# Two edits in the expert loops of a two-block transformer kernel: the order in which u and v are asked for, and the order of a tile's score products

## The chip, the core and the metric

The kernel runs on one core of a Trainium2 chip. The metric is the device time of one execution in microseconds (us), lower is better. The core has five engines with instruction streams of their own: TensorE (PE, matmuls), VectorE (DVE), ScalarE (ACT), GpSimd (POOL) and SyncE (SP), which here issues all transfers. They wait for each other by semaphores. Each engine works its stream off in order, SyncE's queue too: a transfer whose wait has not ended holds up all transfers behind it.

## What is computed

The reference runs two blocks over 256 tokens of width 1024 in float32. Nearly half of the kernel's time, and all of the change, lies in the expert layers ("PEER") of the second block, which has two:

```python
def block(x_t):
    q = jnp.einsum('td,dhk->thk', x_t, w_q).reshape(T, PEER_HEADS, 2, PEER_HALF)
    s = jnp.einsum('thpk,hpnk->thpn', q, sub_keys).astype(jnp.float32)
    sv, si = lax.top_k(s, K)
    ...
    gate = jax.nn.softmax(fv, axis=-1)
    u = u_emb[eidx]
    v = v_emb[eidx]
    act = jax.nn.gelu(jnp.einsum('thkd,td->thk', u, x_t).astype(jnp.float32), approximate=False)
    return jnp.einsum('thk,thkd->td', (gate * act).astype(x_t.dtype), v)
```

Each token picks 8 x 16 of 16384 experts. The kernel does not gather: it computes the scores of all 16384 experts, multiplies them by a gate that is zero where an expert was not picked, and adds up all values. The 16384 experts are 128 tiles of 128, and a tile has two matrices of 128 x 1024 float32 (512 KB), u for the scores and v for the values.

## The kernel before

To keep float32's precision with rounded operands (fp32r), each operand is split into a high part (the rounded copy) and a low part (the rest), and a product is made of high x high, high x low and low x high.

The first 26 tiles of a layer (EARLY) get their scores ahead of time. From tile 26 on, all engines run a software pipeline, written as a loop of six tiles (STEP) a turn. For tile j:

- TensorE: `expert_scores(j)` (L813) makes 16 matmuls into one PSUM bank. L819 multiplies u's high part by both parts of the activations at once (512 columns, the "merged" product), L820 u's low part by their high part (256 columns). `expert_values(j)` (L823) makes 12 matmuls of 512 columns by `in_parts` (L507). The order is scores of j+1, values of j, scores of j+2, values of j+1, and so on. The end of scores adds 1 to `expert_scored`, the end of values adds 1 to `expert_used`.
- ScalarE: after scores of j it stores half of them (L1229), makes the high part of u of tile j+2 when that has landed (L1232), applies Gelu to tile j (L1234), and, when the values of j-1 have ended and v of j+1 has landed, makes the high part of that v (L1238).
- VectorE: the low part of v (L1832), the sum of the two halves of the scores (L1922), the low part of u of j+2 (L1832), and the product with the gate and its split into two parts (L1929, L1828, L1832), which lets the values of j start.
- SyncE: u and v have three slots each (E_SLOTS). u of tile n waits until the scores of n-3 are done (L2189) and is issued at L2190, v of tile n waits until the values of n-3 are done (L2196) and is issued at L2197. The low part of u is written in place of u and read by the scores, so the end of scores is what frees the slot.

The order of the transfers is written out by hand in `load_experts` (L2178), and the order in which TensorE multiplies in `expert_scores`.

Of the kernel before, what the change touches and what calls it, by code (L numbers as in the profile page):

```python
# [18 lines left out]
P = 128  # L19
D = 1024  # L20
KT = D // P
# [11 lines left out]
TILES = NKEYS  # L33
# [16 lines left out]
E_SLOTS = 3  # L50
STEP = 6
# [10 lines left out]
EARLY = CHOICE_TILES + GATE_TILES  # L62
# [55 lines left out]
def low_in_place(n):  # L118

    return n == 0 or n >= EARLY - 2  # L120
# [4 lines left out]
def program(nc, d, out):  # L125
    ctx = ExitStack()
    with ctx:
# [5 lines left out]
        def sem(name):  # L133
            if name not in sems:
                sems[name] = ctx.enter_context(nc.semaphore(name))
            return sems[name]
# [48 lines left out]
        def r3(a, n):  # L185
            return a.rearrange("p (a b) -> p a b", a=n)
# [224 lines left out]
        n = 0  # L411
# [79 lines left out]
        def _(pe):  # L491
# [236 lines left out]
            def experts(l):  # L728
# [24 lines left out]
                for h in range(HEADS8):  # L753
                    if h < PLAIN_HEADS:
                        name, j = ("pq", l, h // 2), h % 2
# [57 lines left out]
                def expert_scores(j, ready):  # L813

                    pe.wait_ge(sem("expert_u"), ready)
                    t = ps[:, 4 + j % 2, :]
                    for k in range(KT):
                        c = slice(k * P, (k + 1) * P)
                        pe.matmul(r3(t, 2), exp_uh[:, j % 2, c], ht_both[:, :, k, :], start=(k == 0), stop=False)  # L819
                        mm = pe.matmul(t[:, 0:T], exp_ul[:, j % E_SLOTS, c], ht_high[:, k, :], start=False, stop=(k == KT - 1))  # L820
                    mm.then_inc(sem("expert_scored"), 1)

# [13 lines left out]
                base = l * TILES  # L836
                for n in range(EARLY - 1):
                    expert_values(n, base + n + 1, first=(n == 0), low=None if low_in_place(n) else exp_uh[:, n % 2])
                    if n == G2_AT:
# [3 lines left out]
                        mm.then_inc(sem("g2_spread"), 1)  # L843
                pe.wait_ge(sem("ht_split"), l + 1)
                expert_scores(EARLY, l * LATE + 1)
                expert_values(EARLY - 1, base + EARLY)
                turns = (LATE - 2) // STEP
                with pe.Fori(0, turns) as i:
                    for j in range(STEP):
                        n = EARLY + j  # L850
                        expert_scores(n + 1, i * STEP + (l * LATE + j + 2))
                        expert_values(n, i * STEP + (base + n + 1))
                for n in range(EARLY + turns * STEP, TILES):
                    if n + 1 < TILES:
                        expert_scores(n + 1, l * LATE + n + 2 - EARLY)
                    expert_values(n, base + n + 1, last=(n == TILES - 1))
# [1301 lines left out]
        def _(sp):  # L2158
# [18 lines left out]
            def load_experts(l):  # L2177
                base = l * TILES  # L2178
                base_v = l * (TILES + 1)
                u, v = d["experts_u"][l], d["experts_v"][l]  # L2180

                def fetch_early(n):
                    if n >= P_SLOTS:
                        sp.wait_ge(sem("expert_scored"), base + n - P_SLOTS + 1)
                    sp.dma_start(pre_u[:, n % P_SLOTS], u[n]).then_inc(sem(f"early_u{n % P_SLOTS}_arrived"), 16)

                def fetch_u(s, src, free=None):
                    if free is not None:
                        sp.wait_ge(sem("expert_scored"), free)  # L2189
                    sp.dma_start(exp_u[:, s, :], src).then_inc(sem(f"expert_u{s}_arrived"), 16)  # L2190

                def fetch_v(s, src, free=None, split=None):
                    if split is not None:
                        sp.wait_ge(sem("expert_v"), split)
                    if free is not None:
                        sp.wait_ge(sem("expert_used"), free)  # L2196
                    sp.dma_start(exp_v[:, s, :], src).then_inc(sem(f"expert_v{s}_arrived"), 16)  # L2197

                def chunk_read(i):
                    s, v = released[("pq", l, i)]  # L2200
                    sp.wait_ge(s, v)

                chunk_read(1)
                chunk_read(2)
                U_AT = [FIRST + GATE_TILES + E_SLOTS + i for i in (0, 2, 4)]
                for n in range(P_SLOTS // 2):
                    fetch_early(n)
                chunk_read(3)
                for n in range(P_SLOTS // 2, P_SLOTS):
                    fetch_early(n)  # L2210
                for n in range(E_SLOTS):
                    fetch_v(n, v[VALUES[n]])
                for n in range(P_SLOTS, EARLY):
                    fetch_early(n)
                for n in range(E_SLOTS, EARLY):
                    if low_in_place(n - E_SLOTS):
                        fetch_v(n % E_SLOTS, v[VALUES[n]], base_v + n - E_SLOTS + 2)
                    else:
                        fetch_v(n % E_SLOTS, v[VALUES[n]], split=base + n - E_SLOTS + 1)
                    if n in U_AT:  # L2220
                        j = EARLY + U_AT.index(n)
                        sp.wait_ge(sem("early_read"), l + 1)
                        fetch_u(j % E_SLOTS, u[j])
                turns = LATE // STEP - 1
                for n in range(EARLY, EARLY + STEP):
                    if n >= EARLY + E_SLOTS:
                        fetch_u(n % E_SLOTS, u[n], base + n - E_SLOTS + 1)
                    if n - E_SLOTS < EARLY - 2:
                        fetch_v(n % E_SLOTS, v[n], split=base + n - E_SLOTS + 1)
                    else:  # L2230
                        fetch_v(n % E_SLOTS, v[n], base_v + n - E_SLOTS + 2)
                with sp.Fori(1, turns + 1) as i:
                    for j in range(STEP):
                        n, s = EARLY + j, (EARLY + j) % E_SLOTS
                        at_ = bass.ds(i * STEP + n, 1)
                        fetch_u(s, u[at_].rearrange("o p n -> (o p) n"), i * STEP + (base + n - E_SLOTS + 1))
                        fetch_v(s, v[at_].rearrange("o p n -> (o p) n"), i * STEP + (base_v + n - E_SLOTS + 2))
                sp.wait_ge(sem("expert_used"), (l + 1) * (TILES + 1))

            def load_keys(l):  # L2240
# [21 lines left out]
            for i in range(2, len(STREAM)):  # L2262
                name = STREAM[i]
                if name == ("evs",):
                    sp.wait_ge(sem("x_ready"), X_READY["end1"])
                    sp.dma_start(pool_mat.rearrange("p s g t -> p (s g t)"), d["pool"]).then_inc(sem("pool_mat"), 16)
                    sp.dma_start(tri_2, d["masks"][:, 4 * T:4 * T + P]).then_inc(sem("pool_mat"), 16)
                if name == ("evs",):
                    for _ in range(BLOCKS_BEHIND[("pool",)]):
                        fetch_block()  # L2270
                    load_keys(0)
                if name == ("od", SLOTS):
                    sp.wait_ge(sem("x_ready"), X_READY["peer_0"])
                    load_keys(1)
                if name == ("wcq",):
                    sp.wait_ge(sem("stored"), STORED["cv"])
                    sp.dma_start(c_row, d["c_row"]).then_inc(sem("c_loaded"), 16)
                load(i)
                for _ in range(BLOCKS_BEHIND.get(name, 0)):
                    fetch_block()  # L2280
                if name in (("pq", 0, 3), ("pq", 1, 3)):
                    load_experts(name[1])
                if name == ("pq", 0, 3):
                    sp.dma_start(causal_3.rearrange("p b k -> p (b k)"), d["masks"][:, 0:2 * T]).then_inc(sem("consts3"), 16)
                    sp.dma_start(inv_f, d["inv_f"]).then_inc(sem("consts3"), 16)
                    sp.dma_start(lam_in.rearrange("p a n -> p (a n)"), d["lam"]).then_inc(sem("consts3"), 16)
# [128 lines left out]
```

## Time and profile before

| | |
|---|---|
| time, median of 3 runs | 2500.53 us (2499.58 to 2501.54) |
| the profiled execution | 2501.91 us, its span 2500.1 us |
| granted TensorE clock | 0.991 of full speed |
| busy | PE 2392.6 us, DVE 1777.2, ACT 1018.3, POOL 298.8 |
| HBM read | 427.66 MB, 171 GB/s over the span |

The span goes from the first to the last instruction. Start times of matmuls are recorded, their ends are modelled: a matmul's recorded duration reaches past the start of the next, so the step from start to start tells the throughput. Times on a timeline are us from the start of the span. PEld is the load of weights, which overlaps matmuls.

### The profile page before, as it was taken

The page shows a single profiled execution, that of the slowest core. Times are in us where ns is not written, and L with a number is a line of the kernel's source. Part 1 is how long each engine was busy: PE and PEld are TensorE (multiplying, and loading weights), DVE is VectorE, ACT ScalarE, POOL GpSimd, SP SyncE. Part 2 cuts the span into 40 slices and gives each one's busy share as a digit, 9 for nine tenths or more (in the row PEclk, how much of TensorE's full clock was granted, in tenths as well). Part 3 has the DMA queues.
Part 4 walks back from the last instruction along what each step waited for, and adds up shares of the span by engine and source line. Part 5 has one row for each costly group of instructions (what it writes and reads, how often), then busy time and mean ns, then how long its engine had stood idle before and what let it go on. Part 6 is the DMA issues. An engine that isn't in the chain of part 4 may idle for free.

```text
span 2500.1 us, 35824 instructions
## 1 busy us (share of the span) xinstructions
PE 2392.6 (96%) x12736; PEld 1973.6 (79%) x12736; DVE 1777.2 (71%) x3774; ACT 1018.3 (41%) x1568; POOL 298.8 (12%) x228
## 2 busy tenths in 40 slices
PE   8998999999999999999999998999999999999997
PEld 7766997678887877887788676798877778788886
DVE  5445887769998666666666756499986666666666
ACT  4433333132334444444444445323344444444443
POOL 0000000045760000000000000366700000000000
PEclk9999999999999999999999999999999999999999
DMA  7324888934215445445455550242164545455443
GB/s 271 140 93 149 322 316 311 374 153 160 68 52 194 176 169 183 178 176 185 173 180 184 200 181 22 101 144 77 36 217 144 184 168 184 170 183 185 178 176 125
DMA packets 97731, 430.07 MB, mean 172 GB/s; under 512 B 11232, under 2 KB 11872, under 8 KB 90720
## 3 DMA queue, kind: packets, MB, share of 16 engines
q1 hardware_dynamic: 97632, 428.75, 47.6%
q8 instruction: 62, 1.02, 0.2%
q14 instruction: 37, 0.30, 0.0%
HBM read 427.66 MB, written 1.05 MB: 171 GB/s over the span
## 4 chain that ended last, share of the span: by engine, by line
PE 56%; DVE 18%; DMA 15%; ACT 5%; issue 4%; SPq 1%; DVEq 0%; ACTq 0%; PEldq 0%
PE ps L507 34%; DMA ring<-in_experts_u 14%; PE ps L552 5%; PE ps L775 4%; DVE HN L1814 4%; PE ps L819 3%; ACT ring_rounded L1232 3%; DVE ring_rounded L1832 3%; DVE HN L1812 3%; PE ps L565 2%; DVE ring L1929 2%; PE ps L820 2%; PE ps L602 1%; DVE ring_rounded L1828 1%; SPq L2197 1%
## 5 line engine op out<-in xcount | busy, mean ns | idle before, releaser
L1832 DVE TENSOR_TENSOR ring_rounded<-ring,ring_rounded 128x1024 fp32r<-128x1024 f32 (+1 forms) x688 | 643.3, 959 | 382.7 <-ACT ring_rounded L1232 356.8
L507 PE MATMUL ps<-ring_rounded 128*128 128x512 f32 x3072 | 760.9, 398 | 35.5 <-DVE ring_rounded L1832 32.0
L507 PEld LDWEIGHTS ps<-ring_rounded 128*128 128x128 f32 x3072 | 558.8, 188 | 201.5 <-DVE ring_rounded L1832 71.7
L819 PE MATMUL ps<-HNHT_rounded,ring_rounded 128*128 128x512 f32 x1632 | 582.6, 397 | 0.0
L820 PE MATMUL ps<-HNHT_rounded,ring_rounded 128*128 128x256 f32 x1632 | 457.4, 280 | 0.0
L819 PEld LDWEIGHTS ps<-HNHT_rounded,ring_rounded 128*128 128x128 f32 x1632 | 306.6, 188 | 73.3
L1232 ACT ACTIVATE ring_rounded<-ring 128x1024 fp32r<-128x1024 f32 x200 | 212.1, 1061 | 341.4 <-DMA ring<-in_experts_u 341.4
L820 PEld LDWEIGHTS ps<-HNHT_rounded,ring_rounded 128*128 128x128 f32 x1632 | 307.8, 189 | 7.9
L507 PE MATMUL ps<-parts 128*128 128x256 f32 (+2 forms) x1184 | 249.2, 301 | 2.6 <-DVE parts L1398 1.5
L1238 ACT ACTIVATE ring_rounded<-ring 128x1024 fp32r<-128x1024 f32 x202 | 212.0, 1049 | 10.7 <-PE ps L507 10.2
L775 PE MATMUL ps<-HT,ring 128*128 128x256 f32 x832 | 202.7, 381 | 1.4 <-ACT arena L985 1.4
L507 PEld LDWEIGHTS ps<-parts 128*128 128x128 f32 x1184 | 192.1, 189 | 13.0 <-issue 2.3
L1229 ACT ACTIVATE ring<-ps 128x256 f32<-128x256 f32 x204 | 78.5, 385 | 287.1 <-PE ps L820 287.1
L2139 POOL TENSOR_TENSOR ring_rounded<-ring,parts 128x1024 fp32r<-128x1024 f32 x8 | 18.8, 2371 | 1400.7 <-ACT parts L1161 1400.7
L2153 POOL TENSOR_SCALAR HN<-iota,slots_t 128x128 f32<-128x128 f32 x128 | 178.1, 1395 | 63.5 <-DVEq L1804 36.3
L985 ACT ACTIVATE arena<-ps 128x512 f32<-128x512 f32 (+4 forms) x136 | 77.2, 580 | 222.4 <-PE ps L507 145.8
L507 PE MATMUL ps<-parts,ring_rounded 128*128 128x256 f32 x576 | 162.4, 282 | 0.0
L775 PEld LDWEIGHTS ps<-HT,ring 128*128 128x128 f32 x832 | 149.0, 192 | 16.6 <-ACT arena L985 1.8
L1403 DVE TENSOR_TENSOR ring_rounded<-ring,parts 128x4096 fp32r<-128x4096 f32 (+2 forms) x28 | 117.5, 4198 | 46.9 <-ACT parts L1008 46.4
L801 PEld LDWEIGHTS ps<-HN 128*128 128x128 f32 x1024 | 131.5, 194 | 23.9 <-issue 10.5
L801 PE MATMUL ps<-HN 128*128 128x128 f32 x1024 | 140.6, 281 | 7.2 <-DVE HN L1814 5.8
L1008 ACT ACTIVATE parts<-ring 128x4096 fp32r<-128x4096 f32 (+2 forms) x28 | 96.5, 3446 | 103.8 <-PE ps L507 85.9
(258 smaller groups left out, 2828.9 us busy)
## 6 DMA issues: line engine op xcount, KB each, us to landing
ring<-in_experts_u SPq DMA_DIRECT2D x256, 512.0 KB, 4.2
ring<-in_experts_v SPq DMA_DIRECT2D x256, 512.0 KB, 3.5
ring<-in_stream SPq DMA_DIRECT2D x45, 2048.0 KB, 8.8
arena<-in_ada SPq DMA_DIRECT2D x96, 512.0 KB, 7.2
arena<-in_keys SPq DMA_DIRECT2D x2, 1024.0 KB, 13.7
ring<-in_stream SPq DMA_DIRECT2D x1, 1792.0 KB, 7.5
ring<-in_stream SPq DMA_DIRECT2D x1, 1664.0 KB, 8.3
ring<-in_stream SPq DMA_DIRECT2D x1, 1040.0 KB, 19.2
```

The costliest lines, as they stand in the source:

```text
L507: mm = pe.matmul(out_, p, q, start=(first and i == 0), stop=(last and i == 2))
L552: mm = pe.matmul(t[:, 0:n], src[:, k, b * P:(b + 1) * P], w[:, k, :], start=(k == 0), stop=(k == nk - 1))
L775: mm = pe.matmul(ps[:, 4 + n % 2, 0:T], pre_u[:, n % P_SLOTS, k * P:(k + 1) * P], HT[:, k, :], start=(k == 0), stop=(k == KT - 1))
L801: mm = pe.matmul(ps[:, 6 + u, t * P:(t + 1) * P], hot[:, u, 1, t, :], hot[:, u, 0, t, :], start=True, stop=True)
L819: pe.matmul(r3(t, 2), exp_uh[:, j % 2, c], ht_both[:, :, k, :], start=(k == 0), stop=False)
L820: mm = pe.matmul(t[:, 0:T], exp_ul[:, j % E_SLOTS, c], ht_high[:, k, :], start=False, stop=(k == KT - 1))
L1232: act.activation(exp_uh[:, j % 2], exp_u[:, (j + 2) % E_SLOTS], ACT.Copy).then_inc(sem("u_high"), 1)
L1238: act.activation(exp_vh[:, (j + 1) % 2], exp_v[:, (j + 1) % E_SLOTS], ACT.Copy).then_inc(sem("v_high"), 1)
L1403: dve.tensor_tensor(weights_low(name), weights(name)[:, 0:IN_PARTS_SIZE[name]], weights_high(name).bitcast(F32), ALU.subtract).then_inc(se ...
L1814: ins = dve.tensor_scalar(hot[:, u, 1, t, :], iota, slots_t[:, 1, at_ + t:at_ + t + 1], slots_t[:, 2, at_ + t:at_ + t + 1], ALU.is_equal, ...
L1832: return dve.tensor_tensor(dst, src, h.bitcast(F32), ALU.subtract)
L2153: pool.tensor_scalar(hot[:, g % 2, 1, GROUP - 1, :], iota, slots_t[:, 1, t:t + 1], slots_t[:, 2, t:t + 1], ALU.is_equal, ALU.mult).then_in ...
```

## The change

In `expert_scores`, the two matmuls of a step of the loop over k become two loops: eight merged products, then the eight of u's low part. In `load_experts`, each step asks for u of tile n and then for v of tile n-1, where it asked for u and v of the same tile; the last v has a place of its own behind the loop. All waits keep their meaning: u of n waits for the scores of n-3, v of n for the values of n-3.

```diff
                     for k in range(KT):
                         c = slice(k * P, (k + 1) * P)
                         pe.matmul(r3(t, 2), exp_uh[:, j % 2, c], ht_both[:, :, k, :], start=(k == 0), stop=False)
+                    for k in range(KT):
+                        c = slice(k * P, (k + 1) * P)
                         mm = pe.matmul(t[:, 0:T], exp_ul[:, j % E_SLOTS, c], ht_high[:, k, :], start=False, stop=(k == KT - 1))
                     mm.then_inc(sem("expert_scored"), 1)
...
                 for n in range(EARLY, EARLY + STEP):
                     if n >= EARLY + E_SLOTS:
                         fetch_u(n % E_SLOTS, u[n], base + n - E_SLOTS + 1)
-                    if n - E_SLOTS < EARLY - 2:
-                        fetch_v(n % E_SLOTS, v[n], split=base + n - E_SLOTS + 1)
-                    else:
-                        fetch_v(n % E_SLOTS, v[n], base_v + n - E_SLOTS + 2)
+                    m = n - 1
+                    if EARLY <= m < EARLY - 2 + E_SLOTS:
+                        fetch_v(m % E_SLOTS, v[m], split=base + m - E_SLOTS + 1)
+                    elif m > EARLY:
+                        fetch_v(m % E_SLOTS, v[m], base_v + m - E_SLOTS + 2)
                 with sp.Fori(1, turns + 1) as i:
                     for j in range(STEP):
-                        n, s = EARLY + j, (EARLY + j) % E_SLOTS
-                        at_ = bass.ds(i * STEP + n, 1)
-                        fetch_u(s, u[at_].rearrange("o p n -> (o p) n"), i * STEP + (base + n - E_SLOTS + 1))
-                        fetch_v(s, v[at_].rearrange("o p n -> (o p) n"), i * STEP + (base_v + n - E_SLOTS + 2))
+                        n, m = EARLY + j, EARLY + j - 1
+                        fetch_u(n % E_SLOTS, u[bass.ds(i * STEP + n, 1)].rearrange("o p n -> (o p) n"), i * STEP + (base + n - E_SLOTS + 1))
+                        fetch_v(m % E_SLOTS, v[bass.ds(i * STEP + m, 1)].rearrange("o p n -> (o p) n"), i * STEP + (base_v + m - E_SLOTS + 2))
+                fetch_v((TILES - 1) % E_SLOTS, v[TILES - 1], base_v + TILES - E_SLOTS + 1)
                 sp.wait_ge(sem("expert_used"), (l + 1) * (TILES + 1))
```

SyncE's order just ahead of and at the head of layer 0's loop over turns of six tiles. The rows of u wait for `expert_scored`, those of v for `expert_used` or, the first of a layer, for VectorE's low part (`expert_v`). First before:

```order
L2197 DMA ring<-in_experts_v 128x1024 [waits expert_v] x5
L2197 DMA ring<-in_experts_v 128x1024 [waits expert_used] x2
L2190 DMA ring<-in_experts_u 128x1024 [waits expert_scored]
L2197 DMA ring<-in_experts_v 128x1024 [waits expert_used]
L2190 DMA ring<-in_experts_u 128x1024 [waits expert_scored]
```

and of the change, at the same place and at the end of the loop:

```order
L2199 DMA ring<-in_experts_v 128x1024 [waits expert_v] x5
L2199 DMA ring<-in_experts_v 128x1024 [waits expert_used]
L2192 DMA ring<-in_experts_u 128x1024 [waits expert_scored]
...
L2192 DMA ring<-in_experts_u 128x1024
L2199 DMA ring<-in_experts_v 128x1024 [waits expert_used]
L2235 REGISTER_ALU
L2235 COMPARE_AND_BRANCH
L2199 DMA ring<-in_experts_v 128x1024 [waits expert_used]
```

Inside the loop both still read u, v, u, v; what moved is that two v stood ahead of the first u that waits and one does now, so that each v is that of the tile before, and one v more stands behind the loop.

TensorE's order inside its loop, from one tile's scores over the values (L507) to the next tile's scores. Before:

```order
L819 MATMUL ps<-HNHT_rounded,ring_rounded 128x512
L820 MATMUL ps<-HNHT_rounded,ring_rounded 128x256
L827 REGISTER_ALU
L507 MATMUL ps<-ring_rounded 128x512 x12
L815 REGISTER_ALU
```

and of the change:

```order
L819 MATMUL ps<-HNHT_rounded,ring_rounded 128x512 x8
L822 MATMUL ps<-HNHT_rounded,ring_rounded 128x256 x8
L829 REGISTER_ALU
L507 MATMUL ps<-ring_rounded 128x512 x12
L815 REGISTER_ALU
```

The first two rows of before stand there eight times in turn; they have become two rows of eight. The values and the place of the waits are the same.

## Rows read from the trace of the kernel before

**Rows 1.** The page, parts 1 and 4: busy time; the last chain by line.
```profile
PE 2392.6 (96%) x12736; PEld 1973.6 (79%) x12736; DVE 1777.2 (71%) x3774; ACT 1018.3 (41%) x1568; POOL 298.8 (12%) x228
...
PE ps L507 34%; DMA ring<-in_experts_u 14%; PE ps L552 5%; PE ps L775 4%; DVE HN L1814 4%; PE ps L819 3%; ACT ring_rounded L1232 3%; DVE ring_rounded L1832 3%; DVE HN L1812 3%; PE ps L565 2%; DVE ring L1929 2%; PE ps L820 2%; PE ps L602 1%;
```

**Rows 2.** Windows: each layer's first to last scores, then two neighbouring tiles of layer 0.
```profile
812.89:1399.34 586.45, 574.22 (x2804) 469.37 (x2803) 395.88 (x596) 271.29 (x400) 0.00 (x0) 1.00 0.50 178
1884.22:2477.59 593.37, 578.71 (x2832) 474.18 (x2830) 400.89 (x604) 274.23 (x403) 0.00 (x0) 1.00 0.50 176
1001.56:1007.51 5.95, 5.84 (x29) 4.69 (x28) 3.96 (x6) 3.16 (x6) 0.00 (x0) 1.00 0.52 176
1007.51:1013.10 5.59, 5.59 (x29) 4.70 (x28) 3.97 (x6) 2.27 (x4) 0.00 (x0) 1.00 0.51 188
```

**Rows 3.** Waits, stretch of layer 0: us in total, times, longest us.
```profile
ACT ring_rounded L1232 <- DMA ring<-in_experts_u: 172.0, 99, 2.6
...
PEld ps L507 <- DVE ring_rounded L1832: 33.1, 72, 1.5
PE ps L507 <- DVE ring_rounded L1832: 10.5, 27, 1.1
```

**Rows 4.** SyncE's queue waits, the same stretch (all it lists).
```profile
SPq L2197 <- PE ps L507: 482.5, 99, 7.0
```

**Rows 5.** The last chain in order of time: start us, us, what.
```profile
1004.64 3.04 PE ps L507 x12
1007.70 0.33 SPq L2197
...
1008.23 4.29 DMA ring<-in_experts_u
1012.54 1.07 ACT ring_rounded L1232
...
1016.25 3.02 PE ps L507 x12
```

**Rows 6.** Timeline of TensorE, one tile and the next one's start.
```profile
1007.51 0.39 PE L819 MATMUL ps<-HNHT_rounded,ring_rounded 128*128 128x512 f32 x1
1007.74 0.28 PE L820 MATMUL ps<-HNHT_rounded,ring_rounded 128*128 128x256 f32 x1
1007.85 0.40 PE L819 MATMUL ps<-HNHT_rounded,ring_rounded 128*128 128x512 f32 x1
...
1010.32 2.94 PE L507 MATMUL ps<-ring_rounded 128*128 128x512 f32 x12
1013.10 0.39 PE L819 MATMUL ps<-HNHT_rounded,ring_rounded 128*128 128x512 f32 x1
```

**Rows 7.** Timeline of ScalarE, its store of half a score and copy of v.
```profile
1010.52 0.39 ACT L1229 ACTIVATE ring<-ps 128x256 f32<-128x256 f32 x1 [1.69 <-PE ps L820]
...
1013.81 1.04 ACT L1238 ACTIVATE ring_rounded<-ring 128x1024 fp32r<-128x1024 f32 x1
```

**Rows 8.** Timeline of TensorE, 256-column matmuls of rounded operands in a row.
```profile
1622.17 0.40 PE L507 MATMUL ps<-parts,HNHT_rounded 128*128 128x256 f32 x2
1622.41 0.29 PE L507 MATMUL ps<-parts,ring_rounded 128*128 128x256 f32 x1
1622.53 0.41 PE L507 MATMUL ps<-parts,HNHT_rounded 128*128 128x256 f32 x2
```

**Rows 9.** Line L820's weight loads: duration ns min/median/max.
```profile
L820 PEld LDWEIGHTS ps<-HNHT_rounded,ring_rounded x1632: 187/188/192, 813.0 to 2480.1; 128*128 128x128 f32 x182
```

**Rows 10.** DMA issues, 900 to 1300 us: KB, us to landing.
```profile
ring<-in_experts_v SPq DMA_DIRECT2D x69, 512.0 KB, 3.5
ring<-in_experts_u SPq DMA_DIRECT2D x68, 512.0 KB, 4.3
```

**Rows 11.** DMA issues, 600 to 700 us, an earlier stage.
```profile
ring<-in_experts_u SPq DMA_DIRECT2D x16, 512.0 KB, 3.5
```

## The prediction

> **What bounds the kernel now.** I read the page first. TensorE has a busy share of 96%, but the chain that ended last spends 14% of the span on the transfer of an expert tile's u part and only some 5% on the two score lines L819 and L820 [rows 1]. An engine that alone set the time would have a chain of its own lines. So the expert loops had to be read tile by tile.
>
> Each layer has 102 tiles from number 26 on, and so 101 periods from the first tile's scores to the last one's. Those stretches take 586.45 and 593.37 us, 1179.8 us together, for 202 periods: 5.84 us a tile [rows 2]. In the same rows stand one tile of 5.59 us, in which TensorE is busy without a hole, and the one ahead of it of 5.95 us. Nothing in the program makes two neighbouring tiles different, so 5.59 us is what TensorE's own work takes, and the 0.25 us above it on average is waiting: 1179.8 - 202 x 5.59 = 50.6 us in all.
>
> The list of waits agrees on the cause and not on the size. ScalarE waits for the transfer of u in 99 tiles of the first stretch, 1.7 us each, and TensorE waits for VectorE at L507 only 10.5 us in sum [rows 3]. That number is too low because the ends of matmuls in the record are modelled (a matmul of 0.39 us stands where the next starts 0.23 us later [rows 6]), and so part of a hole is covered; the weight loads show 33.1 us of the same wait. I therefore take the sum from the periods and not from the idle time.
>
> Why u is late: SyncE has waited 482.5 us in that stretch at L2197, for TensorE's values, and has no row of a wait at L2190 [rows 4]. So v's wait is what holds the queue, and when it ends u's is long fulfilled. The chain of one window shows the circle: values start at 1004.64, v is asked for at 1007.70, u right behind at 1008.23, it takes 4.29 us, ScalarE starts its rounded copy of u (L1232) at 1012.54, and the values two tiles on start at 1016.25 [rows 5]. The circle is 11.61 us for two tiles, 5.81 a tile, more than TensorE's 5.59. Landings that come a little later than others lengthen it further, which gives 5.84 on average.
>
> **The change part by part: the queue.** The transfers are the same number and size; in each step u of tile n now stands ahead of v of n-1. In TensorE's order the scores of n-3, whose end u(n) waits for, stand right ahead of the values of n-4, whose end v(n-1) waits for, and behind those come the scores of n-2. So waits and order now agree, and neither holds up the other. v is asked for at the same event as before, so it costs nothing. u is asked for as soon as its slot's scores are done.
>
> How much earlier that is: TensorE goes from scores to values at 1010.32 [rows 6] and ScalarE, which waits for the same event, starts at 1010.52 [rows 7], so the event is seen 0.2 us later. One undisturbed period earlier it is seen at 1010.52 - 5.59 = 1004.93, where u was in fact asked for at 1008.23: 3.3 us gained. With a landing of 4.3 us, the median in the loop where v is in flight beside it [rows 10], it is there at 1009.2. ScalarE can use it once its store of 0.39 us is done, at 1010.91. So u comes 1.7 us before it is wanted, where now it comes 1.63 us after. Where u travels alone, in an earlier stage, the landing takes 3.5 us [rows 11], and the lead is 2.5 us. I take the longer landing; both are enough.
>
> What is late next: ScalarE's copy of u to the start of values takes 1016.25 - 1012.54 = 3.71 us (its Gelu, VectorE's product and split lie in it) [rows 5]. From 1010.91 that gives 1014.62, and TensorE gets there at 1010.32 + 5.59 = 1015.91: a reserve of 1.29 us. v is asked for at 1007.70, lands after 3.5 us [rows 10] at 1011.2, and ScalarE's copy of it starts only at 1013.81 [rows 7], 2.6 us later. So TensorE is the only bound left and the late landings (the longest wait for u is 2.6 us, 0.9 above the mean [rows 3]) fall into a reserve of 1.7 + 1.3 us. Value of this part: -50.6 us. If one tile in twelve kept a hole of 0.1 to 0.2 us and the first tiles after each entry kept theirs, that would be about 2 us back. Bounds: nothing gained (0) if another wait took its place at once, and -50.6.
>
> **The order inside the scores.** It removes and adds no matmul: eight of 512 columns, then eight of 256, instead of pairs. A tile's scores take 1010.32 - 1007.51 = 2.81 us, in steps of 0.23 to 0.24 and 0.11 us [rows 6]. Matmuls of 512 behind each other, the tile's twelve values, take 2.78 us, 0.232 each [rows 6]. Matmuls of 256 of this type behind each other show three in 0.36 us, 0.120 each [rows 8]. New sum: 8 x (0.232 + 0.120) = 2.82 us, against 2.81: nothing. It lies wholly on TensorE's path, so errors count for all 204 tiles. Lower bound: the 256s keep 0.11 us, 2.74 a tile, -14 us. Upper bound: weight loads, recorded at 0.188 us each [rows 9], stop hiding behind 256 columns, 8 x (0.232 + 0.188) = 3.36 us, +0.55 a tile, +112 us. I take 0, since [rows 8] is the very case, loads included. The values wait for their first weights no differently.
>
> **A rule that speaks against the queue's part.** A pair in flight together takes from 1007.70 to 1008.23 + 4.29, 4.8 us for 1 MB; two that travel alone take 3.5 us each, 7.0 us, more than a period. The Trainium skill ("DMA: Bandwidth & Descriptors", section Bandwidth) advises batches of 1 MiB and more to get near peak rate, and this change takes a pair of half that size apart. This case's rows agree that the pair is the more efficient form. But the queue waits only for TensorE and never for a landing, so the transfers may still overlap, as the pair's 4.8 us shows. With overlap the sum below stands; if they exclude each other, rival (e) gives the time, 2735 us.
>
> **Sum.** Against the profiled execution (2501.91 us, span 2500.1): 2501.9 - 50.6 + 2 + 0 = 2453.3. The median of the runs is 1.4 us below the profiled one, so 2452 us. All outside the two stretches, 1320 us, stays.
>
> **Rivals.**
> (a) Forecast, 2452 us, chance 0.78.
> (b) The next chain takes over in part, chance 0.14. ScalarE or VectorE would need more than the 4.3 us from the scores' event to the values. For it: VectorE is busy 68% of the loop [rows 2] and does its work in a fixed order, and ScalarE's copy of v, which waits for the values' end, stands ahead of its next store. Against: the 1.29 us of reserve. It decides only from there; a chain of 5.72 us in place of 4.3 would leave 0.13 us a tile, half of the gain: 2476 us.
> (c) No change, chance 0.04: u lands no earlier although asked for earlier, or the periods above 5.59 us are TensorE's own. Against it: SyncE's wait [rows 4] and tiles of 5.59 us in both layers. 2500 us.
> (d) Slower through weight loads, chance 0.03. If the scores cost +112 us and the queue gives back 50.6, it is 2562 us. It decides from 0.25 us a tile, that is when a matmul of 256 behind its like costs above 0.11 + 0.03 = 0.14 us. Against it: 0.120 [rows 8].
> (e) Slower through transfers that exclude each other, chance 0.01: 7.0 us a tile instead of 5.84 is +234 us, 2735 us. Against: the pair's 4.8 us shows that they overlap.
>
> **How the numbers follow.** The measurement tells about 0.2%, 5 us, from no change. Faster is (a) and (b), 0.92; same (c), 0.04; slower (d) and (e), 0.04. The range goes down by most of the lower bound of the scores (-14), to 2440, and up to (b) at 2477; it leaves out (c) to (e) and the outer parts.
>
> **What would show it.** After: ScalarE's wait for u, 172 us, nearly gone; SyncE waits at both lines; u asked for at the start of values and v at their end, some 3 us apart, and u's landing nearer 3.5 us; stretches of about 565 us each, tiles of 5.59 us nearly throughout; scores of 2.81 us with steps of 0.23 and 0.12. Wrong would be: scores above 2.9 us without a wait, ScalarE waiting for v instead, or TensorE at L507 still waiting for VectorE in most tiles.

## The result and the profile after

| | before | after |
|---|---|---|
| median | 2500.06 us (4 runs) | 2429.26 us (2428.45 to 2430.41, 4 runs) |
| ratio, 95% interval | | 0.972 [0.9703, 0.9736] |
| profiled span | 2500.1 us | 2427.9 us |

The change makes the kernel 71 us faster. The forecast was 2452 us with a range from 2440 to 2477. The time lies 11 us below the range, and the gain is 1.5 times what I had worked out. The queue's part was right in its cause; the part on the order of the scores, which I had put at nothing, is what took the time out of the range.

The page of the changed kernel, beside [rows 1]: busy time, the share of the DMA engines in 40 slices, the chain that ended last by line, and the two kinds of transfer with their median time to landing.

```profile
PE 2345.9 (97%) x12736; PEld 1975.7 (81%) x12736; DVE 1799.5 (74%) x3774; ACT 1013.8 (42%) x1568; POOL 297.8 (12%) x228
...
DMA  7414788863215565655656551232155555655653
...
PE ps L507 43%; PE ps L819 15%; PE ps L822 8%; PE ps L552 5%; PE ps L775 4%; DVE HN L1816 4%; DVE HN L1814 3%; PE ps L565 2%; PE ps L602 1%; PE ps L623 1%; DVE arena L1826 1%; DVE ring_rounded L1834 1%; PE ps L737 1%; DMA ring<-in_stream 1%
...
ring<-in_experts_u SPq DMA_DIRECT2D x256, 512.0 KB, 3.5
ring<-in_experts_v SPq DMA_DIRECT2D x256, 512.0 KB, 3.4
```

The chain no longer holds a transfer of u (14% before); L507 and the two score lines have become 66% of the span. u lands after 3.5 us over the whole kernel, where it took 4.2.

The two stretches from the first to the last tile's scores, beside [rows 2] (us, then busy time of PE, PEld, DVE, ACT, POOL, the clock, the share of the DMA engines, GB/s):

```profile
812.21:1369.17 556.96, 556.96 (x2832) 475.89 (x2830) 414.59 (x605) 271.53 (x403) 0.00 (x0) 1.00 0.59 188
1848.47:2405.43 556.96, 556.96 (x2831) 475.89 (x2830) 409.78 (x605) 271.65 (x403) 0.00 (x0) 1.00 0.58 188
```

TensorE is busy through all of both, 2 x 556.96 us for 202 periods, 5.514 us a tile. In those rows the DMA engines are busy 0.59 and 0.58 of the time for 188 GB/s, where it was 0.50 for 178. The requests are spread out now, and for the same rate the engines show more busy time; why that is, no run here separates. The rule of the Trainium skill that the prediction weighed ("DMA: Bandwidth & Descriptors", section Bandwidth) is about the size of one transfer. That size is 512 KB before and after, so the rule does not explain the difference. The transfers do not exclude each other: the two landings of a tile, 3.5 and 3.4 us, are 6.9 us together in a period of 5.51. And TensorE waits for none of them.

Beside [rows 3], who waits in layer 0's stretch, and beside [rows 4], the waits of SyncE's queue over the whole kernel:

```profile
ACT ring L1231 <- PE ps L822: 166.3, 101, 1.8
ACT ring_rounded L1240 <- PE ps L507: 117.1, 100, 1.2
DVE ring L1924 <- ACT ring L1231: 81.5, 101, 2.6
```

```profile
SPq L2199 <- PE ps L507: 531.9, 204, 38.5
SPq L2192 <- PE ps L822: 465.7, 198, 4.6
```

The wait for u, 172.0 us before, is not in the list at all. What ScalarE waits for now is TensorE. SyncE waits at both lines, 465.7 us of it for the scores, in place of none. Its timeline shows u, v, u 2.6 and 2.9 us apart:

```profile
1002.88 0.33 SPq L2192 DMA_DIRECT2D ring<-in_experts_u  x1
1005.48 0.33 SPq L2199 DMA_DIRECT2D ring<-in_experts_v  x1
1008.39 0.33 SPq L2192 DMA_DIRECT2D ring<-in_experts_u  x1
```

TensorE's timeline, beside [rows 6]: scores (L819, L822) and values (L507).

```profile
999.77 1.98 PE L819 MATMUL ps<-HNHT_rounded,ring_rounded 128*128 128x512 f32 x8
1001.59 1.12 PE L822 MATMUL ps<-HNHT_rounded,ring_rounded 128*128 128x256 f32 x8
1002.54 2.91 PE L507 MATMUL ps<-ring_rounded 128*128 128x512 f32 x12
1005.29 1.98 PE L819 MATMUL ps<-HNHT_rounded,ring_rounded 128*128 128x512 f32 x8
```

Scores take 1002.54 - 999.77 = 2.77 us, before 2.81; values 1005.29 - 1002.54 = 2.75 us, before 2.78, although no instruction of the values was touched. All tiles are as short: by the starts of single matmuls, 200 of the 202 periods are 5.512 to 5.515 us, and the first of each layer is 5.62. The eight merged products have a step of 1.82 / 8 = 0.227 us, the eight low ones 0.95 / 8 = 0.119. ScalarE works from the scores' end without a hole until it has to wait for the values:

```profile
1002.74 0.38 ACT L1231 ACTIVATE ring<-ps 128x256 f32<-128x256 f32 x1 [1.65 <-PE ps L822]
1003.02 1.05 ACT L1234 ACTIVATE ring_rounded<-ring 128x1024 fp32r<-128x1024 f32 x1
1003.97 0.41 ACT L1236 ACTIVATE ring<-ring 128x256 f32<-128x256 f32 x1
1005.55 1.06 ACT L1240 ACTIVATE ring_rounded<-ring 128x1024 fp32r<-128x1024 f32 x1 [1.17 <-PE ps L507]
```

Its copy of u (L1234) starts 0.48 us after TensorE's turn to the values; before it was 2.22 us [rows 5, 6].

**A correction to my own reading.** The stretch of layer 0 that I took, 812.89 to 1399.34, ends at the scores of the last tile but one. It holds 100 periods and not 101. The whole one is

```profile
812.89:1404.93 592.04, 579.81 (x2832) 474.07 (x2830) 400.79 (x605) 273.41 (x403) 0.00 (x0) 1.00 0.50 177
```

so before, 592.04 + 593.37 = 1185.4 us stood for 202 periods, 5.87 us a tile. 1185.4 - 1113.9 = 71.5 us is nearly the whole difference of the spans (72.2); outside the stretches next to nothing moved.

### The profile page after: what moved, and what is told of

It reads as the page before. It is cut to its first block, busy times and chain, and to the rows that moved or that the text cites. A ratio compares the mean times of both kernels' runs of the same rounds, so it can differ in the third digit from the quotient of the medians.

```text
span 2427.9 us, 35824 instructions
## 1 busy us (share of the span) xinstructions
PE 2345.9 (97%) x12736; PEld 1975.7 (81%) x12736; DVE 1799.5 (74%) x3774; ACT 1013.8 (42%) x1568; POOL 297.8 (12%) x228
## 3 DMA queue, kind: packets, MB, share of 16 engines
HBM read 427.66 MB, written 1.05 MB: 177 GB/s over the span
## 4 chain that ended last, share of the span: by engine, by line
PE 83%; DVE 13%; ACT 2%; DMA 1%; issue 1%; SPq 0%; DVEq 0%; ACTq 0%; PEldq 0%
PE ps L507 43%; PE ps L819 15%; PE ps L822 8%; PE ps L552 5%; PE ps L775 4%; DVE HN L1816 4%; DVE HN L1814 3%; PE ps L565 2%; PE ps L602 1%; PE ps L623 1%; DVE arena L1826 1%; DVE ring_rounded L1834 1%; PE ps L737 1%; DMA ring<-in_stream 1%; PE ps L801 1%
## 5 line engine op out<-in xcount | busy, mean ns | idle before, releaser
L507 PE MATMUL ps<-ring_rounded 128*128 128x512 f32 x3072 | 744.0, 392 | 8.6 <-DVE ring_rounded L1834 8.2
L507 PEld LDWEIGHTS ps<-ring_rounded 128*128 128x128 f32 x3072 | 561.4, 189 | 128.1 <-issue 15.0
L819 PE MATMUL ps<-HNHT_rounded,ring_rounded 128*128 128x512 f32 x1632 | 403.3, 389 | 0.0
L819 PEld LDWEIGHTS ps<-HNHT_rounded,ring_rounded 128*128 128x128 f32 x1632 | 306.2, 188 | 63.4
L507 PE MATMUL ps<-parts 128*128 128x256 f32 (+2 forms) x1184 | 249.2, 301 | 2.3 <-DVE parts L1400 1.5
L822 PEld LDWEIGHTS ps<-HNHT_rounded,ring_rounded 128*128 128x128 f32 x1632 | 222.6, 190 | 15.9
L822 PE MATMUL ps<-HNHT_rounded,ring_rounded 128*128 128x256 f32 x1632 | 227.6, 282 | 0.0
L1924 DVE TENSOR_TENSOR ring<-ps,ring 128x256 f32<-128x256 f32 x204 | 86.6, 424 | 168.7 <-ACT ring L1231 168.7
L1234 ACT ACTIVATE ring_rounded<-ring 128x1024 fp32r<-128x1024 f32 x200 | 210.4, 1052 | 0.0
L507 PEld LDWEIGHTS ps<-parts 128*128 128x128 f32 x1184 | 192.2, 189 | 12.9 <-DVE parts L1400 2.0
L507 PE MATMUL ps<-parts,ring_rounded 128*128 128x256 f32 x576 | 162.4, 282 | 0.0
```

The source lines that it names most:

```text
L507: mm = pe.matmul(out_, p, q, start=(first and i == 0), stop=(last and i == 2))
L1234: act.activation(exp_uh[:, j % 2], exp_u[:, (j + 2) % E_SLOTS], ACT.Copy).then_inc(sem("u_high"), 1)
```

## The experiments

**One half of the change at a time.** The queue's new order with the old scores:

```diff
                         pe.matmul(r3(t, 2), exp_uh[:, j % 2, c], ht_both[:, :, k, :], start=(k == 0), stop=False)
-                    for k in range(KT):
-                        c = slice(k * P, (k + 1) * P)
                         mm = pe.matmul(t[:, 0:T], exp_ul[:, j % E_SLOTS, c], ht_high[:, k, :], start=False, stop=(k == KT - 1))
```

> Only the queue's new order; the scores keep their alternating matmuls. After the result of the change there are 71.5 us to divide, all in the two stretches of 101 periods: 56 us were time above 5.59 us a tile, and 15 us came from a floor that itself fell from 5.59 to 5.51 us (scores 2.81 to 2.77, values 2.78 to 2.75). Theory O, the order of the scores lowered the floor: here tiles stay at 5.59 us, scores at 2.81, the time is 2500 - 56 = 2444 us. Theory Q, the floor fell because transfers and the other engines' work are spread evenly now: here tiles are already 5.51 us, scores about 2.77, and the time is 2429 us. A mix puts the scores' 9 us with the order and the values' 7 us with the queue: 2438 us.

Measured: 2446.86 us, ratio to before 0.9794 [0.9781, 0.9808]. The stretches and one tile of TensorE:

```profile
811.00:1375.93 564.93, 564.93 (x2831) 474.75 (x2830) 417.00 (x605) 271.67 (x403) 0.00 (x0) 1.00 0.59 186
1857.53:2422.54 565.01, 565.01 (x2832) 474.77 (x2830) 412.64 (x605) 271.88 (x403) 0.00 (x0) 1.00 0.59 186
```

```profile
1001.18 0.39 PE L819 MATMUL ps<-HNHT_rounded,ring_rounded 128*128 128x512 f32 x1
...
1003.99 2.94 PE L507 MATMUL ps<-ring_rounded 128*128 128x512 f32 x12
1006.77 0.39 PE L819 MATMUL ps<-HNHT_rounded,ring_rounded 128*128 128x512 f32 x1
```

1129.9 us for 202 periods are 5.594 us a tile, the 5.59 of the prediction in every tile: scores 1003.99 - 1001.18 = 2.81, values 2.78. The queue takes away all waiting and leaves TensorE's own work as it was. Theory O (the order of the scores made TensorE's work shorter) holds. Theory Q (the queue did) falls, and so does the mix: the values are shorter only with the new order too.

The scores' new order with the old queue (`load_experts` as before):

> Only the scores' new order; the queue asks as before. The circle values, v's wait, u's transfer, ScalarE, VectorE, values holds no scores at all, so under the account of the prediction (circle of 11.6 us for two tiles) a faster stream of scores changes nearly nothing: 2494 to 2501 us, with longer holes ahead of the values. Where the order alone already were worth its 9 to 15 us of TensorE time it would be 2485 to 2491 us. In the trace, theory O has every undisturbed scores phase at 2.77 us instead of 2.81; theory Q leaves it at 2.81.

Measured: 2499.01 us, ratio 1.0006 [0.9996, 1.0017]. The stretches, and ScalarE's wait for u in the first:

```profile
812.01:1401.75 589.74, 575.42 (x2831) 480.37 (x2830) 400.62 (x604) 273.85 (x403) 0.00 (x0) 1.00 0.50 178
1882.77:2472.60 589.83, 575.60 (x2831) 480.38 (x2830) 400.15 (x604) 273.55 (x403) 0.00 (x0) 1.00 0.51 178
```

```profile
ACT ring_rounded L1234 <- DMA ring<-in_experts_u: 170.7, 99, 2.6
```

The wait for u is as long as before, and the period is 5.84 us, where it was 5.87; the two profiled executions, 2496.83 and 2501.91 us, differ by no more than runs of one kernel do (the kernel before went from 2492 to 2505 us beside this run). The time that the scores save comes back as longer holes, as a circle without scores in it asks for. Alone this edit gives nothing that can be measured; with the queue mended it gives 1129.9 - 1113.9 = 16.0 us.

**Is the circle the cause?** ScalarE's copy of u in 8 pieces makes just that step of the chain longer. In both kernels:

```diff
-                        act.activation(exp_uh[:, j % 2], exp_u[:, (j + 2) % E_SLOTS], ACT.Copy).then_inc(sem("u_high"), 1)
+                        for piece in range(8):
+                            cut = slice(piece * 128, (piece + 1) * 128)
+                            ins = act.activation(exp_uh[:, j % 2, cut], exp_u[:, (j + 2) % E_SLOTS, cut], ACT.Copy)
+                        ins.then_inc(sem("u_high"), 1)
```

> The changed kernel with ScalarE's rounded copy of u (L1234) cut in 8 pieces of 128 columns, the same numbers. It makes the chain from the scores' end to the values longer by 7 fixed costs of an instruction, some 0.1 us each by the start-to-start times of ScalarE's rows, so 0.7 to 1.0 us. By the account of the prediction a reserve of about 1.2 us stands ahead of the values: the time stays within 0.2% of 2429 us. If the reserve is smaller than that (a rival: TensorE and this chain are nearly even), tiles grow by up to half of the addition, up to 0.4 us or 80 us in all.

> The kernel before with ScalarE's rounded copy of u cut in 8 pieces, the same edit that left the changed kernel at 2428 us and made the copy 0.65 us longer there. In the kernel before the copy lies on the circle v's wait, u's transfer, copy, Gelu, product, values, which decides two tiles at a time. If that circle sets the time, the period grows by 0.65 / 2 = 0.33 us a tile, 66 us in 202 periods: about 2565 us. If instead the holes come only from transfers that land late now and then, with the rest hidden as it is in the changed kernel, it grows by less than 20 us.

Measured: in the changed kernel 2428.12 us, ratio to before 0.9726 [0.9709, 0.9744], the same as without it. In the kernel before it is 2564.54 us, ratio 1.0263 [1.0233, 1.0293], 64 us more, against 66 expected. The copy in the changed kernel (8 pieces, 1.70 us in place of 1.05) and VectorE's wait for it:

```profile
1002.80 1.70 ACT L1236 ACTIVATE ring_rounded<-ring 128x128 fp32r<-128x128 f32 x8
```

```profile
DVE ring_rounded L1837 <- ACT ring_rounded L1236: 114.8, 98, 1.2
```

and the chain of the kernel before with the same copy:

```profile
1006.18 3.04 PE ps L507 x12
1009.77 4.42 DMA ring<-in_experts_u
...
1018.58 1.43 PE ps L507 x5
```

From values to values two tiles on it is 1018.58 - 1006.18 = 12.4 us, where it was 11.61 [rows 5]: 0.65 us from the copy and the rest from a later landing. The same 0.65 us cost 64 / 202 = 0.32 us a tile there, half of the addition because the circle spans two tiles, and nothing in the changed kernel. That is what "on the circle" and "in the reserve" mean, measured with one edit.

The other end of the reserve, the changed kernel with 32 pieces of 32 columns:

> The changed kernel with the rounded copy of u in 32 pieces, by the 0.093 us of a piece's fixed cost 2.9 us longer than in one. The chain from the scores' end to the values is 4.2 us in the changed kernel's trace, so 7.1 us here. A circle of values, scores of the tile after next, chain and its values is then 2.75 + 2.77 + 7.1 = 12.6 us for two tiles, 6.3 a tile against 5.51: +159 us, 2588 us. If the account of the reserve is right, TensorE waits at L507 for VectorE in every tile. If the chain's length did not matter even here, 2429 us.

Measured: 2599.19 us, ratio 1.0394 [1.0368, 1.042]. Its chain:

```profile
1000.16 3.06 PE ps L507 x12
1003.22 1.81 PE ps L819 x8
1005.03 0.97 PE ps L822 x8
...
1006.30 2.72 ACT ring_rounded L1236 x23
...
1009.17 1.06 ACT ring_rounded L1236 x8
...
1012.87 2.34 PE ps L507 x9
```

Values start at 1000.16 and two tiles on at 1012.87: 12.71 us for two tiles, 6.36 a tile, against 6.3 expected. The expectation that TensorE would wait in every tile was wrong: it waits at L507 46 times in the 580 us from 820 to 1400, 91 periods, so in every second tile, and the tile between (its values start at 1005.82) runs without a hole. ScalarE's own work is not the bound either: it still waits 46 times for TensorE's scores there. The circle is in the changed kernel too, without a transfer in it, and it is shorter than TensorE's two tiles by a margin: 0.65 us more fit, 2.9 don't. The margin can be estimated from this chain. The copy's rows took 3.92 us in place of 1.05, so without the pieces the circle is 12.71 - 2.87 = 9.84 us against 11.03 of TensorE, an estimated reserve of 1.2 us, near the prediction's 1.29. No run tested an addition between 0.65 and 2.9 us.

**Where do the 16 us of the order come from?** Scores in blocks of four (merged, low, merged, low):

> The changed kernel with its scores in blocks: four merged products, four of the low part, four merged, four low. It has 3 changes of width inside a tile's scores where the changed kernel has 1 and the kernel before 15. If each change of width costs the same (0.045 us / 14 = 3 ns) the scores take 2.774 us and the time is 1.3 us above the changed kernel's 2429, the same within its noise. If only alternation one by one were costly it is the same too; if only one unbroken row of eight helps, scores are near 2.81 and the time near 2438 us.

Measured: 2437.59 us, ratio 0.9756 [0.9741, 0.9771]; layer 0's stretch and one tile:

```profile
814.20:1374.47 560.27, 560.27 (x2832) 474.93 (x2830) 416.50 (x605) 271.73 (x403) 0.00 (x0) 1.00 0.60 187
...
1000.08 2.93 PE L507 MATMUL ps<-ring_rounded 128*128 128x512 f32 x12
1002.84 1.07 PE L820 MATMUL ps<-HNHT_rounded,ring_rounded 128*128 128x512 f32 x4
1003.75 0.64 PE L823 MATMUL ps<-HNHT_rounded,ring_rounded 128*128 128x256 f32 x4
1004.22 1.09 PE L820 MATMUL ps<-HNHT_rounded,ring_rounded 128*128 128x512 f32 x4
1005.15 0.63 PE L823 MATMUL ps<-HNHT_rounded,ring_rounded 128*128 128x256 f32 x4
1005.62 1.56 PE L507 MATMUL ps<-ring_rounded 128*128 128x512 f32 x6
```

The time is near the last of the three figures, but not for its reason. Scores are 2.78 us, not 2.81, and values 1002.84 - 1000.08 = 2.76. The account by changes of width falls: 3 ns each would be 1.3 us in all, and it was 8 by the medians, 2 x (560.27 - 556.96) = 6.6 by the stretch. The loss lies in both phases. The starts of single matmuls show where. In the changed kernel the medians of the steps in the values are 233, 236, 228, 232, 231 ns and then 227 ns for the rest. A matmul of 512 columns runs at 227 ns only when several of its like stand ahead of it. Behind the row of eight matmuls of 256 it is slower for five steps. The kernel in fours goes back from 256 to 512 columns twice a tile: the four merged products inside the scores have 233, 236, 228 and 232 ns, and behind the second block the values are back at 227 ns only from the tenth step on; the nine before average 232. The changed kernel goes back once a tile. In alternation it happens eight times, cut short each time: there each matmul of 512 in the scores but a tile's first has a step of 232 to 241 ns, and the values are back at 227 only from the eleventh step on; the ten before average 233. Together the medians of a tile are 44 ns more in the scores and 36 ns more in the values than in the changed kernel, 0.080 x 202 = 16.2 us.

To separate the values from what stands ahead of them, the low part went between the first merged product and the other seven:

```diff
+                    pe.matmul(r3(t, 2), exp_uh[:, j % 2, 0:P], ht_both[:, :, 0, :], start=True, stop=False)
                     for k in range(KT):
                         c = slice(k * P, (k + 1) * P)
-                        pe.matmul(r3(t, 2), exp_uh[:, j % 2, c], ht_both[:, :, k, :], start=(k == 0), stop=False)
-                    for k in range(KT):
+                        pe.matmul(t[:, 0:T], exp_ul[:, j % E_SLOTS, c], ht_high[:, k, :], start=False, stop=False)
+                    for k in range(1, KT):
                         c = slice(k * P, (k + 1) * P)
-                        mm = pe.matmul(t[:, 0:T], exp_ul[:, j % E_SLOTS, c], ht_high[:, k, :], start=False, stop=(k == KT - 1))
+                        mm = pe.matmul(r3(t, 2), exp_uh[:, j % 2, c], ht_both[:, :, k, :], start=False, stop=(k == KT - 1))
```

> The changed kernel with the scores as one merged product, the eight of u's low part, then seven merged. Still one return from 256 to 512 columns a tile, now inside the scores and not at the head of the values. Starts from start in the trace of the changed kernel show a matmul of 512 columns at 227 ns in a long row, and at 233, 236, 228, 232, 231 ns in the first five after a matmul of 256. Theory R, the return costs those 25 to 30 ns wherever it stands: values fall from 2.75 to 2.72 us, scores rise by the same from 2.77, and the time is that of the changed kernel, 2429 us within 0.2%. Theory V, the values' first steps are slow for a reason of the values (other operands, another bank): they stay at 2.75 and the scores rise, 2432 to 2438 us.

Measured: 2430.88 us, ratio 0.9729 [0.9704, 0.9754], the changed kernel's within the noise. Layer 0's stretch, 556.92 us where the changed kernel has 556.96, and one tile:

```profile
812.42:1369.34 556.92, 556.92 (x2832) 475.86 (x2830) 412.20 (x605) 271.45 (x403) 0.00 (x0) 1.00 0.59 188
...
999.95 0.39 PE L817 MATMUL ps<-HNHT_rounded,ring_rounded 128*128 128x512 f32 x1
1000.17 1.11 PE L820 MATMUL ps<-HNHT_rounded,ring_rounded 128*128 128x256 f32 x8
1001.12 1.78 PE L823 MATMUL ps<-HNHT_rounded,ring_rounded 128*128 128x512 f32 x7
1002.74 2.88 PE L507 MATMUL ps<-ring_rounded 128*128 128x512 f32 x12
1005.46 0.39 PE L817 MATMUL ps<-HNHT_rounded,ring_rounded 128*128 128x512 f32 x1
```

The values take 1005.46 - 1002.74 = 2.72 us, 0.227 a matmul, and the seven merged products behind the low ones 1.62 us, 0.231 each; their first steps are 233, 236, 228, 233 and 231 ns. Theory R holds: the return from 256 to 512 columns costs some 0.03 us inside the scores as at the head of the values, where other operands and another bank are in use. With one return in either order there was nothing to win, and none of the kernels run beats the changed one.

## Why the prediction was right and where it was wrong

The step that failed is a term of the sum: "The order inside the scores", put at 0, measured at 16.0 us. The queue's part had the right mechanism and was too small by a miscount. Without the 16.0 us the time would have been in the range.

**The bound, the circle and the queue: right.** Holes caused by u, u held up by v's wait, a period of 5.59 us once that is gone: the queue alone gave 5.594 us. u came before it was wanted in every tile, the landing fell to 3.5 us, the copy of v was on time, and the longer copy showed the circle before and the reserve after. The passage on how much earlier u is asked for holds too: 1002.88 is 0.34 us behind the scores' end, not 0.2, well within the lead.

**"1179.8 - 202 x 5.59 = 50.6 us": the count was wrong.** The first stretch had 100 periods. With 1185.4 us the same line gives 56.2 us, and the queue alone measured 1185.4 - 1129.9 = 55.5. The rows themselves would have told: the first stretch has 2804 matmuls and the other 2832, and the difference is 28, the matmuls of one tile. This is 5.6 of the missing 23 us.

**"The order inside the scores: nothing": mis-sized, and too small in scope.** I took 0.232 us for a matmul of 512 in a row from the values' 2.78 us. But those values stood behind an alternating phase, and their first steps carried its cost. Clean, it is 0.227 us, and the new scores are 8 x (0.227 + 0.119) = 2.77. The price of a 256 in a row, 0.120 by [rows 8], was right. The second half is what I left out: I priced the scores alone, as if their order could not touch the values behind them, and the values became faster by 0.03 us. Together that is 16.0 us where I had 0. My lower bound of -14 us rested on another idea (cheap matmuls of 256) and came near by accident; the range then took only most of it.

**The 2 us of remaining holes** did not come: with the new queue all tiles but the first of a layer have the same length. No row had shown that term.

Put together: 2452 - 5.6 - 16.0 - 2 = 2428.4 us, measured 2429.3.

Of the rivals, (b) was refuted by the trace after, in which the values wait in no tile, and the 8 pieces showed that a reserve was left; (c) was refuted by the queue alone, (d) and (e) by the trace after. The price in (b) was also doubled: it counts what the chain is too long by in full for every tile, but the circle spans two, and in the two kernels where it was made to set the time the loss was about half of the excess. The upper end of the range, 2477 us, hangs on that price. The rival that I lacked is a gain of TensorE's own beyond the tile that I had called undisturbed.

## What to carry to other kernels

In a queue that works in order, put transfers in the order in which their slots come free, and not in the pairs in which they are used: here moving each v one place back gave 2.1%. When a row of equal steps is to give the price of an instruction, take its last ones: the first may still carry what stood ahead. And count the periods of a stretch by its instructions before dividing by them. An edit that is worth nothing on a kernel that waits can be worth its full price once the wait is gone, so two edits have to be measured alone and together.

## What the runs showed of the hardware that I had not expected

A rounded (fp32r) matmul of 512 columns, weights loaded for each, runs at steps of 0.227 us at the full clock (granted 1.00 in these stretches) in a long row, one of 256 at 0.120. The Trainium skill ("TensorE: Matmul & The Clock Gate", section Back-to-back issue gap) gives N / 2.4 + 2.5 ns for the gap of an isolated matmul, about 216 ns for 512 columns; by that formula 256 columns would be 109 ns, an estimate. For a stream with a weight load for each matmul, the case here, the section has about 131 ns for 512 columns. The traces have 227 and 120 ns, and they decide.

After the row of eight matmuls of 256, the next five of 512 have steps of 233, 236, 228, 232 and 231 ns, in the values as in the scores. The first matmul of 256 after a row of 512 steps on after 113 ns, the second after 119, the rest after 120. One would suspect weight loads that run ahead in long matmuls and are used up in short ones. The records do not show that. The load for the next matmul starts 1 to 5 ns after the start of the one before it at all but 2 of the 5656 matmuls of the two stretches, in slow steps as in fast ones, and so never more than one ahead:

```profile
1001.59 0.90 PEld L822 LDWEIGHTS ps<-HNHT_rounded,ring_rounded 128*128 128x128 f32 x7
1002.42 2.60 PEld L507 LDWEIGHTS ps<-ring_rounded 128*128 128x128 f32 x12
1005.06 0.64 PEld L819 LDWEIGHTS ps<-HNHT_rounded,ring_rounded 128*128 128x128 f32 x3
```

The first load for the values starts at 1002.42, 0.12 us ahead of the values and with the last matmul of the scores. What makes the steps behind the short matmuls slow stays open.
